# Where RMSNorm's row factors are applied in a two-layer decoder trunk: on normalised rows, or on what the products give

## The reference, cut to what matters

```python
D_MODEL, SEQ, EPS = 2048, 256, 1e-6
def rmsnorm(x, g):
    y = x * rsqrt(mean(x * x, axis=-1) + EPS)        # one factor per row (token)
    return y * g                                     # one gain per feature

x = x + stick_breaking_attention(rmsnorm(x, sb_norm_g), w_qkv, w_o)     # 16 heads of 128
x = x + peer_ffn(rmsnorm(x, peer_norm_g[0]), w_q[0], keys_1, keys_2, u, v)
# shared latent K/V and the second attention
ckv    = rmsnorm(x, kv_norm_g) @ w_dkv               # 512 latent columns and 64 for rope
c      = rmsnorm(ckv[:, :512], kv_latent_g);  k_rope = rope(ckv[:, 512:])
cq     = rmsnorm(rmsnorm(x, mla_norm_g) @ w_dq, q_latent_g)
x = x + mla_attention(...) @ w_o
x = x + peer_ffn(rmsnorm(x, peer_norm_g[1]), w_q[1], ...)
return rmsnorm(x, final_norm_g)

def peer_ffn(h, ...):        # 8 heads; product keys; 128 experts of 16384 chosen per token
    q = h @ w_q              # scores with two tables of 128 keys, top 16 of each, top 16 of 256
    g = softmax(top_sc)      # per head
    act = gelu(h . u[ids]);  out = sum(g * act * v[ids])
```

## Time and profile before

| what | value |
|---|---|
| median of 3 runs | 4038.1 us (4035.34 to 4038.82) |
| the profiled execution | 4039.92 us, its span 4038.2 us |
| TensorE busy | 3888.5 us, 96% of the span, 20142 matmuls |
| VectorE / ScalarE / GpSimd busy | 2148.8 / 1781.6 / 1026.9 us |
| chain of work that ended last | TensorE 93%, VectorE 3%, issue 2%, ScalarE 1%, GpSimd 1% |
| mean granted TensorE clock | 0.977 |
| moved by DMA | 823.25 MB, mean 204 GB/s |

### The profile page before, as it was taken

How to read it: one execution, slowest core, us unless ns; L and a number is a source line. 1 busy time by engine, 2 the same in 40 slices (tenths; PEclk the granted TensorE clock), 3 DMA queues, 4 the chain that set the end, 5 groups by cost and what they waited for, 6 DMA issues and landing times.

```text
span 4038.2 us, 49124 instructions
## 1 busy us (share of the span) xinstructions
PE 3888.5 (96%) x20142; PEld 3259.2 (81%) x20142; DVE 2148.8 (53%) x2991; ACT 1781.6 (44%) x2124; POOL 1026.9 (25%) x454
## 2 busy tenths in 40 slices
PE   6996999999999999999988898999999999999998
PEld 5885788888888888888867677888888888888886
DVE  4435468777544444444444645887764444444444
ACT  3334434455544444444443343445554444444443
POOL 1224156422122222222211114651112222222221
PEclk9997999999999999999988898999999999999999
DMA  4550445577865766666633234556877566666664
GB/s 178 188 188 32 167 157 197 208 232 233 263 224 212 253 231 239 231 239 231 239 137 130 100 125 148 195 204 212 253 234 252 209 244 240 230 240 230 239 232 164
DMA packets 279152, 823.25 MB, mean 204 GB/s; under 512 B 146064, under 2 KB 178832, under 8 KB 195216
## 3 DMA queue, kind: packets, MB, share of 16 engines
q1 hardware_dynamic: 94176, 682.73, 47.7%
q10 hardware_dynamic: 184752, 137.38, 10.8%
HBM read 750.84 MB, written 69.21 MB: 203 GB/s over the span
## 4 chain that ended last, share of the span: by engine, by line
PE 93%; DVE 3%; issue 2%; ACT 1%; POOL 1%; DMA 0%; DVEq 0%; SPq 0%; POOLq 0%; ACTq 0%
PE bank L1176 30%; PE bank L1175 14%; PE bank L1321 12%; PE bank L1319 12%; PE bank L1317 12%; PE bank L1196 3%; PE bank L1197 3%; PE bank L1198 3%; PE bank L1178 1%; PE bank L1288 1%; PE bank L1289 1%; DVE lo L688 1%; PE bank L1212 1%; DVE act_t L714 1%; PE bank L1237 0%
## 5 line engine op out<-in xcount | busy, mean ns | idle before, releaser
L436 ACT ACTIVATE hi<-raw 128x1024 fp32r<-128x1024 f32 x1294 | 1370.2, 1061 | 1764.9 <-PE bank L1176 763.2
L688 DVE TENSOR_TENSOR lo<-raw,hi 128x1024 fp32r<-128x1024 f32 x887 | 1090.3, 1232 | 1600.2 <-ACT hi L436 1599.7
L1176 PE MATMUL bank<-act_t,hi 128*128 128x512 f32 x5120 | 1784.7, 397 | 5.5 <-DVE act_t L714 5.5
L400 POOL TENSOR_TENSOR lo<-raw,hi 128x1024 fp32r<-128x1024 f32 x407 | 985.5, 2422 | 2935.5 <-ACT hi L436 2935.5
L1175 PE MATMUL bank<-act_t,lo 128*128 128x256 f32 x4800 | 1355.1, 282 | 0.0
L1176 PEld LDWEIGHTS bank<-act_t,hi 128*128 128x128 f32 x5120 | 942.9, 188 | 206.6 <-DVE act_t L714 6.7
L1175 PEld LDWEIGHTS bank<-act_t,lo 128*128 128x128 f32 x4800 | 909.0, 189 | 13.7
L1321 PE MATMUL bank<-hi,wa 128*128 128x512 f32 x2048 | 643.2, 395 | 0.0
L1317 PE MATMUL bank<-hi,wa 128*128 128x512 f32 x2048 | 643.2, 395 | 0.0
L1319 PE MATMUL bank<-lo,wa 128*128 128x512 f32 x2048 | 643.1, 395 | 0.0
L1321 PEld LDWEIGHTS bank<-hi,wa 128*128 128x128 f32 x2048 | 383.8, 187 | 94.0
(11 more groups left out here) (210 smaller groups left out, 2340.7 us busy)
## 6 DMA issues: line engine op xcount, KB each, us to landing
raw<-in_stream SPq DMA_DIRECT2D x647, 1024.0 KB, 4.8
act_rows<-stage ACTq DMA_DIRECT2D x64, 512.0 KB, 4.0
w_rows<-w_stage ACTq DMA_DIRECT2D x64, 512.0 KB, 5.4
acts<-act_rows ACTq DMA_DIRECT2D x64, 512.0 KB, 4.1
w_part<-w_rows ACTq DMA_DIRECT2D x64, 512.0 KB, 5.4
x_res<-in_x SPq DMA_DIRECT2D x2, 1024.0 KB, 6.1
keys_sb<-in_keys ACTq DMA_DIRECT2D x2, 1024.0 KB, 4.8
out<-xn SPq DMA_DIRECT2D x2, 1024.0 KB, 4.0
```

Of the source, the lines that this page charges most:

```text
L400: pool.tensor_tensor(lo[:, s, :], raw[:, n0 % RAW_SLOTS, j * HALF:(j + 1) * HALF], hi[:, s, :].bitcast(F32), ALU.subtract).then_inc(lo_rea ...
L436: act.activation(hi[:, s, :], raw[:, slot, j * HALF:(j + 1) * HALF], ACT.Copy).then_inc(hi_ready[s], 1)
L688: dve.tensor_tensor(lo[:, s, :], raw[:, n0 % RAW_SLOTS, j * HALF:(j + 1) * HALF], hi[:, s, :].bitcast(F32), ALU.subtract).then_inc(lo_read ...
L1176: ins = mm(ps[:], w_hi, act_t[:, kt, :, :].rearrange("p w t -> p (w t)"), start=first, stop=last)
```

## The change: what it does

- `x` is also passed transposed (`x_t`). At the start, `x_t` is loaded in four pieces of 512 KB, times the gain, straight into `act_t`; there is no transpose and no row factor in it. The first two weight units are loaded between these pieces, `x` after them. A unit may start when its first feature tiles stand (`rows=`).
- The row factor is computed later and applied to results: q and k heads are multiplied by `inv_row` (the factor of each token, spread over all partitions by a product of ones with a diagonal matrix, `spread_inverse`), v rows by a per-row factor. The first six heads (`UNSCALED`) are multiplied together once the factor is there. The rope angles are computed at heads 10 and 12.
- In `wo` and `mwo`, the finished column block q-1 of the unnormalised `x_res` is transposed in the middle of the first unit of block q (`turn_block`), and the last one in the middle of the first routing unit. The left side of the output product moves to a tile of its own, `ot_t`, so that `act_t` can be rebuilt meanwhile.
- Routing scores stay unscaled; the factor goes into the exponent of the softmax. Each expert tile's sums are multiplied by `inv_row` on DVE (256 more instructions), and the gelu waits for that.
- For `c`, `rope` and `dq` the gain vectors are multiplied onto the weights as they are split; `act_t` then holds plain `x` once for all three, so `norm_mla` goes. DVE does all these splits, in pieces (two of 512 columns to a half; 16 of 64 in `rope`). The rows are transposed between the units of `c`. The latent norms use eps times the squared row root instead of the factor.
- Banks are assigned anew in `ps_out`, so that the banks of the first two column blocks come free first.

```diff
+def weight_gains(n0):
+    if U0["c"] <= n0 < U0["c"] + 4:
+        return G_KV + 4 * (n0 - U0["c"]), 512
+    if n0 == U0["rope"]:
+        return G_KV, ROPE
+    if U0["dq"] <= n0 < U0["dq"] + 4:
+        return G_MLA + 4 * (n0 - U0["dq"]), 512
+    return None
...
-        ps_out = [[bank[2], bank[3], bank[6], bank[7]], [bank[4], bank[5], bank[0], bank[1]]]
+        ps_out = [[bank[6], bank[7], bank[2], bank[3]], [bank[4], bank[5], bank[0], bank[1]]]
...
         def gpsimd_takes(n0, s):
+            if weight_gains(n0) is not None:
+                return n0 == U0["rope"] and s == HALF_SLOTS - 1
...
# SP
+            load_xt(0)
+            load(0)
+            for i in range(1, XT_PIECES):
+                load_xt(i)
+            load(1)
+            for c in range(NC_TOK):
+                sp.dma_start(x_res[:, c, :], x[c * P:(c + 1) * P, :]).then_inc(x_in, 16)
+                load(2 + c)
+            (positions and inv_freq)
...
# ACT: split_hi
+                    pieces = gain_pieces(n0, j)
+                    if pieces is None:
+                        act.activation(hi[:, s, :], half, ACT.Copy).then_inc(hi_ready[s], 1)
+                    else:
+                        for col, at in pieces:
+                            ins = act.activation(hi[:, s, at], half[:, at], ACT.Copy, scale=gain_t[:, col:col + 1])
...
+            def output_product(phase, rows_phase, col):
                 for q in range(QUARTERS):
+                    first = U0[phase] + 4 * q + LEAD
+                    split_hi(first)
                     if q >= 1:
+                        rows_hi(rows_phase, 2 * q - 2, col)
+                        rows_hi(rows_phase, 2 * q - 1, col)
                         squares(B0[phase], q - 1)
+                    split_range(first + 1, first + 4)
+                rows_hi(rows_phase, KT // 2 - 2, col)
+                rows_hi(rows_phase, KT // 2 - 1, col)
                 squares(B0[phase], QUARTERS - 1)
                 x_norm()
-                gains_hi(norm_phase, KT, col, act_t)
...
# ACT: start
+            for i in range(XT_PIECES):
+                act.wait_ge(xt_landed[i], 16)
+                for f in range(2):
+                    xt_hi(2 * i + f)
+                if i == 0:
+                    split_hi(0)
+            split_range(1, UNSCALED)
             act.wait_ge(x_in, 16 * NC_TOK)
+            root_mean_square(lambda c: x_res[:, c, :], ...)
+            split_range(UNSCALED, ANGLES_AT + 3 + LEAD)
...
# DVE
             def sum_tile(t):
-                    sum_halves(stage[:, t % STAGED, :], a0 + t)
+                    st = stage[:, t % STAGED, :]
+                    sum_halves(st, a0 + t)
+                    dve.wait_ge(a_free, GRANTED + a0 + t + 1)
+                    dve.tensor_tensor(st, st, inv_row[:], ALU.mult).then_inc(scaled, 1)
...
# ACT
             def gelu(t):
-                    act.wait_ge(a_free, GRANTED + a0 + t + 1)
+                    act.wait_ge(scaled, layer * TILES + t + 1)
...
# PE: weights_by_features
                         kt = KT // 2 * j + q
+                        if rows is not None and kt % 2 == 0:
+                            pe.wait_ge(rows[0], rows[1] + kt // 2 + 1)
...
+            def turn_block(phase, b_phase, q):
+                pe.wait_ge(b_free, GRANTED + B0[b_phase] + q + 1)
+                turn_x(phase, 2 * q)
+                turn_x(phase, 2 * q + 1)
+            def spread_inverse(phase, count):
+                pe.wait_ge(inv_diag_ready, count)
+                for c in range(NC_TOK):
+                    ins = mm(ps_c[idx % 2][:, c * P:(c + 1) * P], ones[:], inv_diag[:, c, :], start=True, stop=True)
...
+            def kv_rows(u, j):
+                f = 2 * u + j
+                if f == 0:
+                    turn_kv(0)
+                    turn_kv(1)
+                elif f + 1 < KT // 2:
+                    turn_kv(f + 1)
+                pe.wait_ge(v_added, 2 * QUARTERS)
+                pe.wait_ge(c_free, GRANTED + C0["rows_kv"] + f + 1)
-            norm(3, A0["norm_kv"])
-            block_b(U0["c"], B0["c"], act_t, 4)
+            block_b(U0["c"], B0["c"], by_k_tile(act_t), 4, kv_rows)
...
-            turn_rows(xn, KT, A0["norm_mla"])
```

More of the change, by code:

```diff
@@ L82 @@
 OUT_LAG = 3
+UNSCALED = 6
+ANGLES_AT = 10
+XT_PIECES = 4
 SB_SCALE = 128 ** -0.5
@@ L129, with gain_pieces @@
 N_GAINS = G_LQ + LT
+def weight_gains(n0):
[6 more added lines that the diff above has]
+    return None
+def gain_pieces(n0, j):
+    gains = weight_gains(n0)
+    if gains is None or (n0 == U0["rope"] and j == 1):
+        return None
+    col, width = gains
+    n = HALF // width
+    return [(col + n * j + q, slice(q * width, (q + 1) * width)) for q in range(n)]
 def batch_at(tile):
@@ L155, in sync, with build_program @@
         self.engine.wait_ge(self.semaphore, self.count)
-def build_program(nc, x, positions, stream, keys, gains, final_g, inv_freq, out):
+def build_program(nc, x, x_t, positions, stream, keys, gains, final_g, inv_freq, out):
     with ExitStack() as ctx:
@@ L275, in build_program @@
         boot = sem("boot")
+        gains_in = sem("gains_in")
+        xt_landed = [sem(f"xt_landed{i}") for i in range(XT_PIECES)]
+        xt_ready = sem("xt_ready")
+        inv_ready = sem("inv_ready")
+        inv_diag_ready = sem("inv_diag_ready")
+        heads_scaled = sem("heads_scaled")
+        scaled = sem("scaled")
         x_in = sem("x_in")
@@ L348, in _, with load_xt @@
         def _(sp):
[L349 to L353, removed]
+            sp.dma_start(gain_t[:], gains).then_inc(gains_in, 16)
+            def load_xt(i):
+                kts = slice(i * KT // XT_PIECES, (i + 1) * KT // XT_PIECES)
+                sp.dma_start(xt_in[:, kts, :], x_t[:, kts, :]).then_inc(xt_landed[i], 16)
             def load(n0):
@@ L725, in copy_block, with scale_block @@
                 ins.then_inc(b_free, 1)
+            def scale_block(idx, dst, col, last):
+                unit_done(dve, last)
+                for c in range(NC_TOK):
+                    ins = dve.tensor_scalar(dst[:, c, col:col + 512], ps_b[idx % 2][c][:], stat[:, 2 + c:3 + c], None,
+                                            ALU.mult)
+                ins.then_inc(b_free, 1)
             def add_block(idx, col, last):
@@ L750, in blocks, with output_product @@
                         store(b0 + nb, 512 * nb, last)
+            def output_product(phase, rows_phase, col):
+                first = U0[phase]
+                for q in range(QUARTERS):
+                    for j in range(3):
+                        split_lo(first + 4 * q + j + LEAD)
+                        if j == 0 and q >= 1:
+                            rows_lo(rows_phase, 2 * q - 2, col)
+                            rows_lo(rows_phase, 2 * q - 1, col)
+                    last = first + 4 * q + 3
+                    add_block(B0[phase] + q, 512 * q, last)
+                    split_lo(last + LEAD)
+                rows_lo(rows_phase, KT // 2 - 2, col)
+                rows_lo(rows_phase, KT // 2 - 1, col)
             def rotate(src, dst, c, heads):
@@ L1060, in _ @@
             scale_rows(3, lambda c: ps_b[c_idx % 2][c][:], lambda c: c_tok[:, c, :], 4, xn_ready)
-            dve.wait_ge(xn_ready, 4)
+            dve.wait_ge(xn_ready, 1)
             dve.sem_inc(b_free, 1)
-            gains_lo(A0["norm_mla"], KT, G_MLA, act_t)
-            gains_lo(A0["ct"], LT, G_LKV, c_t)
+            split_lo(U0["rope"] + LEAD)
             unit_done(dve, U0["rope"])
@@ L1162, in _, with weights_by_features @@
             mm = pe.matmul
-            def weights_by_features(n0, ps, middle=None):
+            def weights_by_features(n0, ps, middle=None, rows=None):
                 for j, s, k in halves(n0):
@@ L1444, in _ @@
             pe.wait_ge(b_free, GRANTED + B0["mla"] + HEADS)
-            for nb in range(4):
-                block_b(U0["mwo"] + 4 * nb, B0["mwo"] + nb, act_t, 4)
-            norm(6, A0["norm_p1"])
+            output_product("mwo", "rows_p1")
             routing(1)
```

359 lines of the change are left out of this document (256 added, 103 removed).

## The result

The changed kernel takes 3985.76 us (median of 4 runs, 3980.18 to 3989.07), the kernel before it 4038.19 on the same chip (4 runs): the ratio is 0.9872 [0.9859, 0.9884], a gain of 52 us. I forecast 3956 and a gain of 84, with a range of 3942 to 3981. The direction was right, and the time lies 5 us above the range.

What follows compares the result with a forecast made beforehand. TensorE, busy 96% of the span, was taken as the bound. Gains of 28.3 (start), 18.0 and 17.1 (`wo`, `mwo`) and 24 (latent stage) make 87.4, less 3.5: 84 off 4039.9 gives 3956 us; range 3942 to 3981.

Steps and rivals of the forecast that it cites:

- Expert tiles: Both layers: 256 new DVE multiplications of 0.42 us each, for which PE does not wait; cost taken as 2.5 us.
- The first rival: Routing stretch: DVE becomes the bound as multiplications wait for POOL; 25 us more for PE, 3981 us; chance 0.16.
- The named test: Expert tiles: between 550 and 700 us, PE's waits for DVE stay under 3 us.
- Latent stage: Last `v` product to `kn`: `c` starts 15.6 us earlier, `norm_mla` goes; net gain 24 us, bounds 15 and 28.
- `wo` and `mwo`: Gaps before `wq0` and `wq1` go, 32 transposes stay between products; net gains 18.0 and 17.1 us, bounds 12 and 19 each.
- Start: Kernel start: first product at 10.3 us, first unit done at 18.5; net gain 28.3 us, bounds 24 and 30.
- The wait for the spread product: Start, around head 6: PE's wait there was counted at 0.3 us.
- (1): Routing stretch: DVE becomes the bound, its multiplications waiting for POOL; 25 us more for PE, 3981 us; chance 0.16.
- (2): Latent stage gains 15 us and start 24, pieces of `c`, `rope`, `dq` overloading DVE; 3969 us; chance 0.12.
- (3): `wo` and `mwo`: rows between units make PE wait 2.7 us in six quarters, 16 us; 3972 us; chance 0.07.
- (4): Expert tiles: gelu's longer chain delays ACT's split and PE in every tile, 108 us; slower, 4064 us; chance 0.03.

Runs made afterwards that it cites:

- e2_no_scale: The changed kernel with the multiplication of every expert tile by `inv_row` left out, gelu waiting for the sum alone; 3964.78 us (ratio 0.9821).
- e3_psum_row: The changed kernel with the expert layers' spread inverse kept in PSUM, where the multiplication reads it; 3969.09 us (ratio 0.9834).
- e6_odd64: The changed kernel with the arena's tiles starting at an odd multiple of 64 bytes; 3986.12 us (ratio 0.9872).
- e5_before_align: The kernel before the change with only the arena's start rounded to a multiple of 64 bytes; 3995.68 us (ratio 0.9900).

## Why the prediction was wrong, step by step

**Expert tiles (forecast -2.5, measured -21.7): the step that failed.** Everything needed was in the working: the operation is of the kind that waits for POOL, DVE is full in 694 to 705, the sum comes late there. The first rival took this to 25 us and 3981. I gave it 0.16, and priced the 256 multiplications at 2.5 us, on the sentence "the matches wait for POOL anyway, and a wait moved ahead isn't a second one". It is a second one: the 64 matches took 6.5 us less than before (57.5 against 64.0), the new multiplications waited 115. In the stretch that I called 82% busy and just before it, between 550 and 766, PE now waits 6.4 us for sums and 2.0 for a split of POOL's. The row of the stretch in the changed kernel, against the first of the earlier trace rows:

```profile
616.00:766.00 150.00, 141.56 (x822) 121.70 (x822) 141.70 (x187) 63.14 (x80) 76.87 (x32) 0.99 0.54 190
```

The same with the row in PSUM:

```profile
616.00:766.00 150.00, 147.95 (x883) 127.95 (x882) 132.69 (x175) 69.88 (x88) 77.68 (x31) 1.00 0.58 203
```

DVE rose from 122.3 to 141.7 us of 150 and PE lost 8.4. That DVE had 27.7 us idle there was an average too: the gaps come at single tiles. The one of 1.59 us at 625.94 is behind a split on DVE that took 3.35 us instead of 1.2 (L801 at 621.94, while POOL worked from 621.80 to 624.20), the one of 1.83 at 633.67 behind two steps of the routing on DVE that took 3.99 us beside POOL.

The gaps are 8.4 us of layer 0's 11.5 and 5.9 of layer 1's 10.2. Most of the rest is TensorE's clock, which the forecast did not have there. Behind three of the gaps (2.00 us at 660.60, 1.82 at 2592.74, 2.03 at 2643.99) it fell to the lower level for about 3 us; behind the gaps of 1.59 and 1.83 us it did not. The first 4 us behind the gap at 660.60, and behind the one at 633.67 (the clock is the third figure from the end):

```profile
660.60:664.60 4.00, 4.00 (x14) 3.47 (x15) 3.96 (x4) 0.98 (x2) 4.00 (x2) 0.57 0.00 0
633.67:637.67 4.00, 4.00 (x23) 3.49 (x24) 3.90 (x15) 2.32 (x3) 1.16 (x1) 1.00 0.80 262
```

At the lower level two products take 0.64 us from start to start instead of 0.35, which makes about 1.5 us for each of the three; the first products behind every gap take 0.2 to 0.3 us more than others. The named test, waits for DVE under 3 us in 550 to 700, failed: they are 5.5.

**Latent stage (24, measured 16.7).** The start of `c` (8.2 us after the last `v` product; 8.35) and its length (28.2; 28.4) held. What failed was `rope`: I had the pieces at 0.17 and 0.14 each, they took 0.245 on ACT (3.92 for 16) and 0.20 on DVE (3.22), one chain behind the other; the wait was 4.4 and not 2.4, and I carried the 16.3 us of the products over although they now stood behind a gap. The wait and the products are 2.0 and 4.4, `dq` up to `kn` took 1.3 more than the shorter of my two figures, and start and length of `c` 0.4: 8.1 in all, of which 0.7 was already in the rounding to 24.

**`wo` and `mwo` (18.0 and 17.1, measured 14.4 and 14.0).** The handoffs work as forecast: no gap, transposes at 0.79. Up to the first routing product the forecast was 17.5 and 16.6 (see below the table), so 3.1 and 2.6 are missing. Most of it is a term I did not have: moving the left side to `ot_t` was costed at nothing, and its address makes each of 384 products 6.6 ns dearer, 2.5 us per stage (`mwo` 92.45 against 90.11 with the arena moved). In `wo` the clock at the stage's start adds some 0.5: over its first 8 us it was 0.62 in the profiled execution of the change and 0.70 in that of before, while in e2_no_scale, e3_psum_row and e6_odd64, whose `wo` is that of the change, it was 1.00 and `wo` took 92.5 us and not 95.2, and in e5_before_align, whose `wo` is that of before, 1.00, and 87.3 us and not 89.6. That leaves 0.3 or less in each.

**Start (28.3, measured 27.1).** Right: the first product came 0.8 us later than forecast, the first unit's end 0.2. The wait for the spread product was 1.16 instead of 0.3. ACT at its first table load:

```profile
5.72 1.28 ACT L510 ACT_TABLE_LOAD   x1 [5.72 <-DMA xt_in<-in_x_t]
7.01 1.30 ACT L510 ACTIVATE act_t<-xt_in,gain_t 128x256 fp32r<-128x256 f32 x3
```

The next instruction begins 1.29 us after the load did. The load at 40.91, ahead of the roots, began 0.02 us after ACT's last square ended, and the root follows it 1.30 us later. So here too no drain beside the load is to be seen, and the estimate that I made with a figure of the Trainium skill, "ScalarE: Activation LUTs", "What ACT_TABLE_LOAD costs" (about 3 us less gain), is not borne out.

**Rivals.** (1) was the case, though beside most of the forecast. Its mechanism was right; that its size (25 against 21.7) was near was luck. It let each of the 26 early tiles of a layer cost 1.62 us of DVE, 84 in all; those 52 multiplications took 56.8, only 23 of them held up, and by its own sum the 55 us of idle time would have covered all but 2 of that. 81 of the 115 us of waiting fell behind tile 26. PE lost its time at single tiles and by the clock, which no sum over the stretch has. (2) had the size of the latent term half right (16.7 between its 15 and my 24) but the start was not late. (3) fell: no gap in `wo` or `mwo`. (4) fell: gelu's longer chain did not hold PE, as e3_psum_row keeps the chain and loses most of the waits. The range failed since its upper end took rival (1) alone: 3981 with a full latent stage. Rival (1) with the latent stage at half its way to 15 is 3985.

## What to carry to other kernels

Before adding a VectorE instruction to a stretch where another engine works on SBUF, look at what its kind does there now: the maximum beside the median of a similar line (here 2626 against 416 ns) tells whether it will queue, and each such instruction can queue anew (77 of 256 did here). If it must be there, let one operand come from PSUM. An idle share over 150 us says little of single steps, and a gap of 2 us in TensorE can cost nearly as much again by the clock behind it. When a tile that TensorE reads is moved to another place, its start address is a cost to be checked: the change's 52 us stood beside 44 that one line of address rounding gave.

## What the runs showed of the hardware that was not expected

- The start address of the stationary operand: 226.7 ns per 512-column product at a multiple of 128 bytes, 233.3 at the other two places tried, an odd multiple of 32 and one of 64. In 6144 products of the two `v` stages this is 41 us. What in the engine causes it, no run here shows.
- 64-column products ran down to the lower granted clock within a stage in which PE never paused (0.64, 0.60, 0.70 on the mean in three kernels), and ran wholly at 1.2 GHz when a gap of 4.4 us lay ahead of them.
- TensorE's granted clock fell from 2.4 to 1.2 GHz behind gaps of 1.82, 2.00 and 2.03 us in the expert tiles (0.57 on the mean over the next 4 us), and stayed full behind gaps of 1.59 and 1.83 us. The length of the gap alone doesn't tell which it will be.
- A multiplication that POOL held up ended 0.28 to 0.29 us after POOL's instruction, in all 77 cases, though an unhindered one takes 0.42; why, the rows don't say.
